# Products of the full array split into two row halves that work side by side on two token tiles

## The chip, the cores and the metric

One core of a Trainium2 chip runs the kernel. The metric is the device time of one execution in microseconds (us). The kernel before takes 2042.18 us (median of three runs, 2042.11 to 2042.24). Its engines: TensorE (PE in the rows; PEld is its loading of stationary operands), VectorE (DVE), ScalarE (ACT), GpSimd (POOL) and SyncE (SP), which issues the large transfers.

## The reference

A trunk of two layers over 256 tokens of 2048 numbers in float32, each layer a mixer and an MLP, each with an RMS norm ahead and a residual sum behind:

```python
for layer in range(DEPTH):                       # DEPTH = 2
    h = rmsnorm(x, norm_mix_w[layer])
    if layer % 2 == 0:   # retention (8 heads) and RG-LRU (8 blocks) behind one input product
        y = hybrid_mixer(h, hyb_w_in[e], ..., hyb_w_out[e], pos)
    else:                # windowed attention, 32 query heads, 4 key heads, learned sinks
        y = swa_sink_attention(h, attn_w_qkv[o], attn_sinks[o], attn_w_out[o])
    x = x + y
    h = rmsnorm(x, norm_mlp_w[layer])
    u = jax.nn.relu(h @ w_up)                    # 2048 x 8192
    x = x + (u * u) @ w_down                     # 8192 x 2048
return rmsnorm(x, final_norm_w)
```

Nearly all the arithmetic is weight products of [256 x 2048] by [2048 x 512] pieces.

## The kernel before, in words

**Blocks.** The weight products are cut into 89 blocks (`BLOCKS`): each takes all 2048 rows of contraction and 512 output columns, for both token tiles (`tt` 0 and 1, 128 tokens each). A block is 8 halves (`HALVES`), each half is 256 rows of contraction, two steps `e` of 128 rows: 712 halves in all. The two token tiles accumulate in two banks of PSUM, `acc[:, b % 2, tt]`; the other two of `acc` belong to the neighbouring block.

**Three products for one.** Weights and activations are kept as a high part and a low part in a rounded 32-bit format (`w_hi`, `w_lo`; `a_hi`, `a_lo` or `b_hi`, `b_lo`). Each step is hi x hi, hi x lo and lo x hi (L1040, L1041, L1042). So a half has 2 steps x 2 token tiles x 3 = 12 products, each with a stationary 128x128 piece of the activations and 512 streamed weight columns.

**How a half comes in.** SP loads 1 MB of weights (two halves) into one of four places of `raw` (L420), ACT rounds a half into `w_hi` (`cut_hi`, L537), DVE subtracts to get `w_lo` (`cut_lo`, L722) and raises `lo_ready`. `w_hi` and `w_lo` are rings of four halves (`RING = 4`). `cut_hi` waits for `half_used`, which TensorE raises at the end of each half. ACT and DVE run the same list of slots: in slot `b`, at each position `k` of 0 to 7, first what is left over from block `b - 1` (`post`, `lru`, `retention`, `attention`), then the cut of half `k + 4`. Each engine works strictly in this written order.

**What is left over from a block.** After an "up" block (MLP, first product) ACT takes the sums out, applies ReLU and squares; DVE transposes 32x32 tiles (L908), 4 at position 1 and 6 at each of positions 2 and 3; then ACT and DVE write the high and low parts. After a "res" block DVE adds into `x` and does the same transposes. "down" blocks only add into `x`. In the mixers and in attention TensorE itself transposes (`turn_block`, L1051; L1140) and computes scores and values between the halves (L1084, L1085: gates of the LRU; L1095, L1096: retention's scores; L1105 to L1107: its values; L1130: attention's scores; L1154: its values). These use full rows, except L1130, whose operands have 64 rows and 64 columns, and L1154, with 64 columns. Most of these small ones are plain 32-bit matmuls that the compiler issues as two each. `retention` on DVE waits for the scores at positions 2 and 3 and makes `ret_decayed`; rotation of q and k is L767 to L772.

**The loops.** Six of eight chunks of the two MLPs run in a loop on each engine (`run_slots`); two blocks at the joint from up to down are woven (`WOVEN`, `piece`).

Of the kernel before, what the change touches and what calls it, by code (L numbers as in the profile page):

```python
# [28 lines left out]
P = 128  # L29
# [4 lines left out]
TT = SEQ // P  # L34
# [5 lines left out]
CHUNK = 64  # L40
# [4 lines left out]
LRU_BLOCKS = 8  # L45
LG = LRU_BLOCKS // 2
# [11 lines left out]
UNITS = 4  # L58
HALVES = 8
RING = 4  # L60
# [20 lines left out]
MIX_OUT0 = len(MIX_IN)  # L81
# [4 lines left out]
PERIOD = 2 * COLS  # L86
# [20 lines left out]
def piece(b, k):  # L107


    for first in (b, b - 1):  # L110
        if first in DOWN0:
            d, h = WOVEN[HALVES * (b - first) + k]
            return first + d, h
    return b, k
# [77 lines left out]
def row_groups(b):  # L192


    return [0, 2, 3, 1] if MIX_OUT0 <= b < MIX_OUT0 + COLS else [0, 1, 2, 3]
# [20 lines left out]
def build(nc, t):  # L216
    ctx = ExitStack()
    with ctx:
        def sb(name, shape, dt=F32):
            return ctx.enter_context(nc.sbuf_tensor(name, shape, dt))  # L220

        def sem(name):
            return ctx.enter_context(nc.semaphore(name))
# [3 lines left out]
        w_hi = sb("w_hi", [P, RING, 2, NB], F32R)  # L227
        w_lo = sb("w_lo", [P, RING, 2, NB], F32R)
# [70 lines left out]
        acc = ctx.enter_context(nc.psum_tensor("acc", [P, 2, TT, NB], F32))  # L299
# [13 lines left out]
        hi_ready = sem("hi_ready")  # L313
        lo_ready = sem("lo_ready")
        half_used = sem("half_used")
        evac_act = sem("evac_act")
        evac_dve = sem("evac_dve")
        squared = sem("squared")
# [4 lines left out]
        turned_out = sem("turned_out")  # L323
# [24 lines left out]
        lru_lo = sem("lru_lo")  # L348
# [36 lines left out]
        def stationary(b):  # L385

            from_b = (MIX_OUT0 <= b < MLP0 or ATT_OUT0 <= b < MLP1
                      or BLOCKS[b][0] == "down" or (b >= MLP0 and BLOCKS[b][0] in ("res", "fin")))
            return (b_hi, b_lo) if from_b else (a_hi, a_lo)
# [637 lines left out]
        def _(pe):  # L1027
            def products(slot, k):

                b, h = piece(slot.b, k)  # L1030
                hi, lo = stationary(b)
                pe.wait_ge(lo_ready, slot.halves(k + 1))
                for e in range(2):
                    kt = 4 * row_groups(b)[h // 2] + 2 * (h % 2) + e
                    wh, wl = w_hi[:, k % RING, e, :], w_lo[:, k % RING, e, :]
                    first, last = h == 0 and e == 0, h == HALVES - 1 and e == 1
                    for tt in range(TT):
                        xh, xl = (s[:, kt, tt * P:(tt + 1) * P] for s in (hi, lo))
                        a = acc[:, b % 2, tt, :]
                        nc.tensor.matmul(a, xh, wh, start=first, stop=False)  # L1040
                        nc.tensor.matmul(a, xh, wl, start=False, stop=False)  # L1041
                        ins = nc.tensor.matmul(a, xl, wh, start=False, stop=last)  # L1042
                ins.then_inc(half_used, 1)

            def turn_block(src, banks):

                for m in range(2):
                    for e in range(2):
                        for tt in range(TT):
                            c = (2 * m + e) * P  # L1050
                            ins = nc.tensor.transpose(  # L1051
                                bank[:, banks + m, e * SEQ + tt * P:e * SEQ + (tt + 1) * P],
                                src[:, tt, c:c + P], ident[:, :])
                    ins.then_inc(turned, 1)

            def post(slot):

                b = slot.b - 1
                kind, j = BLOCKS[b]
                if kind not in TURNED - BY_QUADRANT:  # L1060
                    return
                if kind in FROM_STAGE:
                    pe.wait_ge(evac_act, slot.count(N_EVAC_ACT, 0))
                    src = stage
                elif kind in "qk":
                    pe.wait_ge(rotated, {("q", 0): 1, ("k", 0): 2, ("q", 1): 3, ("k", 1): 4}[(kind, j)])
                    src = turn
                else:
                    pe.wait_ge(gated, TT * (j + 1))
                    pe.wait_ge(ret_evac, TT * (j + 1))  # L1070
                    src = turn
                if kind == "aq" and j > 0:
                    pe.wait_ge(att_lo, TT * j)
                pe.wait_ge(turned_out, slot.count(N_TURNED, -1, INIT_HALVES))
                turn_block(src, 0)
# [35 lines left out]
            def retention(half, k):  # L1111
                for what, h in {1: [(ret_score, 0), (ret_score, 1)],
                                2: [(ret_value, 0), (ret_score, 2), (ret_value, 1), (ret_score, 3)],
                                3: [(ret_value, 2), (ret_value, 3)]}.get(k, []):
                    what(half, h)
# [43 lines left out]
            def attention(g, k):  # L1159
                late = att_late(g)  # L1160
                for what, tt in {1: [(att_scores, 0)], 2: [(att_scores, 1)],
                                 4 + late: [(att_turn, 0), (att_turn, 1)],
                                 5 + late: [(att_value, 0), (att_value, 1)]}.get(k, []):
                    what(g, tt)
# [11 lines left out]
            def body(slot):  # L1176
                b = slot.b
                if b == NBLK:
                    return
                if b >= 2:  # L1180

                    if BLOCKS[b - 2][0] in BY_ACT:
                        pe.wait_ge(evac_act, slot.count(N_EVAC_ACT, -1))
                    else:
                        pe.wait_ge(evac_dve, slot.count(N_EVAC_DVE, -1))
                if b in STATIONARY_STARTS:
                    pe.wait_ge(turned_out, slot.count(N_TURNED, -1, INIT_HALVES))
                for k in range(HALVES):
                    if b == 0:
                        pe.wait_ge(turned_out, k + 1)  # L1190
                    if b == MIX_OUT0 and k in (2, 5):
                        pe.wait_ge(lru_lo, LRU_BLOCKS - 1 + k // 5)
                    if b == ATT_OUT0 and k == 0:
                        pe.wait_ge(att_lo, TT * (KV - 1))
                    if b == ATT_OUT0 and k == HALVES - 2:
                        pe.wait_ge(att_lo, TT * KV)
                    if b in STATIONARY_STARTS - DOWN0 and k == HALVES - 2:
                        pe.wait_ge(turned_out, slot.count(N_TURNED, 0, INIT_HALVES))
                    if b in DOWN0 and k == HALVES - 2:
                        pe.wait_ge(evac_act, slot.count(N_EVAC_ACT, 0))  # L1200
                    if b - 1 in DOWN0 and k == HALVES - 4:
                        pe.wait_ge(turned_out, slot.count(N_TURNED, -1, INIT_HALVES))
                    products(slot, k)
                    if b == 0 and k == 5:

                        pe.wait_ge(vecs_loaded, 144)
                        pe.wait_ge(turned_out, INIT_HALVES)
                        nc.tensor.transpose(bank[:, 2, 0:4 * KT], vec_rows[0:4 * KT, 0, :], ident[0:4 * KT, 0:4 * KT])
                        nc.tensor.transpose(bank[:, 2, 4 * KT:136], vec_rows[0:72, 1, :],
                                            ident[0:72, 0:72]).then_inc(vecs_turned, 1)  # L1210
                    if b == 0 and k in (1, 3):
                        j = 2 + k // 2
                        pe.wait_ge(x_loaded[j], 16)
                        pe.wait_ge(turned_out, 2 * (j - 1))
                        turn_block(x[:, :, j * NB:(j + 1) * NB], 2 * (j % 2))
                    if b > 0:
                        kind, j = BLOCKS[b - 1]
                        if k == TURN_AT.get(kind):
                            post(slot)
                        if slot.i is None:  # L1220
                            if kind == "v":
                                retention(j, k)
                            if b in LRU_IN_SLOT and k == 4:
                                lru_gates(LRU_IN_SLOT[b])
                            if kind == "aq":
                                attention(j, k)

            run_slots(pe, body)


# [22 lines left out]
```

## Time and profile before

| | |
|---|---|
| median of 3 runs | 2042.18 us |
| the profiled execution | 2042.25 us, span 2040.4 us |
| PE busy | 2006.0 us, 98% |
| PEld busy | 1655.3 us, 81% |
| DVE busy | 1422.7 us, 70% |
| ACT busy | 1019.6 us, 50% |
| POOL busy | 43.3 us, 2% |
| DMA | 187 GB/s over the span |

A matmul's recorded duration (0.39 us for a product) includes its way through the array; a stream of them starts one every 0.227 us, so the busy times overlap. The time between starts is the cost of one in a stream.

### The profile page before, as it was taken

Reading aid. Unit: us, or ns where it says so; the run is one execution under the profiler, and the core shown is the slowest. Engines: PE = TensorE matmul, PEld = TensorE weight load, DVE = VectorE, ACT = ScalarE, POOL = GpSimd, SP = SyncE. Lnnn points to the kernel's source line nnn. Section 1 sums busy time; section 2 is a strip of 40 time slices with the busy share of each in tenths; the row PEclk is TensorE's granted clock in tenths of the full one; section 3 lists DMA queues with packets and bytes.
Section 4 is the critical chain, followed back from the end, with each engine's and each line's share of the span. In section 5 each row is a group of like instructions: output and inputs, shape, how many; then the busy total and the mean of one; then the engine's idle time right before and its main releaser. Section 6 shows DMA issues by size and latency. Waiting matters only on the chain.

```text
span 2040.4 us, 24588 instructions
## 1 busy us (share of the span) xinstructions
PE 2006.0 (98%) x9195; PEld 1655.3 (81%) x9195; DVE 1422.7 (70%) x1931; ACT 1019.6 (50%) x1343; POOL 43.3 (2%) x55
## 2 busy tenths in 40 slices
PE   8999999999999999999999999999999999999997
PEld 6888888878888888888887877878888888888876
DVE  5776678887567657756888677978548756855864
ACT  5566665555345435434555554555445434534543
POOL 1110110000000000000000000000000000000000
PEclk9999999999999999999999999999999999999999
DMA  8556546656656665556656544566656566566552
GB/s 292 171 169 210 175 156 208 198 171 206 194 180 204 198 192 189 201 186 194 197 173 199 165 133 156 181 193 192 200 188 195 193 191 196 182 204 193 186 192 97
DMA packets 191612, 382.49 MB, mean 187 GB/s; under 512 B 6184, under 2 KB 6448, under 8 KB 191408
## 3 DMA queue, kind: packets, MB, share of 16 engines
q1 hardware_dynamic: 190288, 377.58, 57.1%
q0 software_dynamic: 1216, 3.88, 0.5%
q8 instruction: 49, 0.80, 0.2%
q14 instruction: 27, 0.22, 0.0%
q10 hardware_dynamic: 32, 0.01, 0.0%
HBM read 379.34 MB, written 2.10 MB: 187 GB/s over the span
## 4 chain that ended last, share of the span: by engine, by line
PE 89%; DVE 6%; ACT 3%; issue 1%; DMA 0%; ACTq 0%; SPq 0%; DVEq 0%
PE acc L1040 29%; PE acc L1042 29%; PE acc L1041 29%; DVE w_lo L722 2%; DVE turn L908 2%; ACT w_hi L537 1%; PE bank L1051 1%; PE bank L1130 0%; DVE a_lo L734 0%; ACT L601 0%; PE bank L1140 0%; PE bank L1154 0%; ACT area L627 0%; DMA x<-in_x 0%; ACT L607 0%
## 5 line engine op out<-in xcount | busy, mean ns | idle before, releaser
L722 DVE TENSOR_TENSOR w_lo<-raw,w_hi 128x1024 fp32r<-128x1024 f32 x712 | 867.1, 1225 | 550.5 <-ACT w_hi L537 548.0
L537 ACT ACTIVATE w_hi<-raw 128x1024 fp32r<-128x1024 f32 x712 | 748.2, 1059 | 835.6 <-PE acc L1042 835.3
L1040 PE MATMUL acc<-w_hi,a_hi 128*128 128x512 f32 x1568 | 616.3, 393 | 5.0 <-DVE a_lo L734 4.7
L1042 PE MATMUL acc<-w_hi,a_lo 128*128 128x512 f32 x1568 | 611.2, 390 | 0.0
L1041 PE MATMUL acc<-w_lo,a_hi 128*128 128x512 f32 x1568 | 611.0, 390 | 0.0
L1040 PE MATMUL acc<-w_hi,b_hi 128*128 128x512 f32 x1280 | 499.0, 390 | 4.9 <-DVE b_lo L730 2.6
L1042 PE MATMUL acc<-w_hi,b_lo 128*128 128x512 f32 x1280 | 498.0, 389 | 0.0
L1041 PE MATMUL acc<-w_lo,b_hi 128*128 128x512 f32 x1280 | 498.0, 389 | 0.0
L1040 PEld LDWEIGHTS acc<-w_hi,a_hi 128*128 128x128 f32 x1568 | 295.0, 188 | 68.8 <-DVE a_lo L734 6.0
L1042 PEld LDWEIGHTS acc<-w_hi,a_lo 128*128 128x128 f32 x1568 | 294.8, 188 | 61.9
L1041 PEld LDWEIGHTS acc<-w_lo,a_hi 128*128 128x128 f32 x1568 | 295.0, 188 | 60.1
L1040 PEld LDWEIGHTS acc<-w_hi,b_hi 128*128 128x128 f32 x1280 | 240.3, 188 | 56.4 <-DVE b_lo L730 3.5
L1042 PEld LDWEIGHTS acc<-w_hi,b_lo 128*128 128x128 f32 x1280 | 240.3, 188 | 50.2
L1041 PEld LDWEIGHTS acc<-w_lo,b_hi 128*128 128x128 f32 x1280 | 240.3, 188 | 49.6
L908 DVE STREAM_TRANSPOSE turn<-stage 32x256 f32<-32x256 f32 x512 | 223.1, 436 | 7.7
L545 ACT ACTIVATE b_hi<-turn 128x512 fp32r<-128x512 f32 x64 | 37.0, 625 | 101.1 <-DVE turn L908 101.1
L908 DVE STREAM_TRANSPOSE turn<-x 32x256 f32<-32x256 f32 x192 | 83.6, 436 | 2.9
L582 ACT ACTIVATE stage<-acc,rinv 128x512 f32<-128x512 f32 x92 | 57.6, 674 | 1.4 <-DVE rinv L755 1.4
L929 DVE TENSOR_TENSOR x<-x,acc 128x512 f32<-128x512 f32 x80 | 51.1, 680 | 8.6 <-PE acc L1042 8.6
L730 DVE TENSOR_TENSOR b_lo<-turn,b_hi 128x512 fp32r<-128x512 f32 x64 | 41.2, 685 | 0.0
L587 ACT ACTIVATE stage<-stage 128x512 f32<-128x512 f32 x64 | 36.7, 627 | 0.0
L555 ACT ACTIVATE junk<-x 128x512 f32<-128x512 f32 x40 | 25.0, 624 | 11.8 <-DVE x L929 11.1
(152 smaller groups left out, 522.6 us busy)
## 6 DMA issues: line engine op xcount, KB each, us to landing
raw<-in_mlp_w_up SPq DMA_DIRECT2D x128, 1024.0 KB, 5.6
raw<-in_mlp_w_down SPq DMA_DIRECT2D x128, 1024.0 KB, 5.1
raw<-in_hyb_w_in SPq DMA_DIRECT2D x48, 1024.0 KB, 5.1
raw<-in_attn_w_qkv SPq DMA_DIRECT2D x20, 1024.0 KB, 5.1
raw<-in_hyb_w_out SPq DMA_DIRECT2D x16, 1024.0 KB, 5.3
raw<-in_attn_w_out SPq DMA_DIRECT2D x16, 1024.0 KB, 5.1
x<-in_x SPq DMA_DIRECT2D x4, 512.0 KB, 9.7
out_y<-x SPq DMA_DIRECT2D x4, 512.0 KB, 4.0
```

The source lines that it names most:

```text
L537: nc.scalar.activation(w_hi[:, h % RING], raw[:, h // 2, 2 * (h % 2):2 * (h % 2) + 2, :], ACT.Copy).then_inc(hi_ready, 1)
L545: nc.scalar.activation(hi[:, kt:kt + 2, :], src, ACT.Copy).then_inc(turned_hi, 1)
L555: nc.scalar.activation(junk[:, :], x[:, tt, j * NB:(j + 1) * NB], ACT.Square, accum_out=sums[:, norm, tt, j:j + 1]).then_inc(summed, 1)
L582: ins = nc.scalar.activation(stage[:, tt, :], src, ACT.Relu if kind == "up" else ACT.Copy, scale=s)
L587: nc.scalar.activation(stage[:, tt, :], stage[:, tt, :], ACT.Square).then_inc(squared, 1)
L722: nc.vector.tensor_tensor(w_lo[:, h % RING], raw[:, h // 2, 2 * (h % 2):2 * (h % 2) + 2, :], w_hi[:, h % RING].bitcast(F32), ALU.subtract) ...
L730: nc.vector.tensor_tensor(lo[:, kt:kt + 2, :], src, hi[:, kt:kt + 2, :].bitcast(F32), ALU.subtract).then_inc(turned_out, 1)
L908: ins = nc.vector.transpose(dst[f * QUAD:(f + 1) * QUAD, :, :, a, :], src[a * QUAD:(a + 1) * QUAD, :, :, f, :])
L929: nc.vector.tensor_tensor(xs, xs, acc[:, b % 2, tt, :], ALU.add).then_inc(evac_dve, 1)
L1040: nc.tensor.matmul(a, xh, wh, start=first, stop=False)
L1041: nc.tensor.matmul(a, xh, wl, start=False, stop=False)
L1042: ins = nc.tensor.matmul(a, xl, wh, start=False, stop=last)
```

## The change

`products` is called for even `k` only and handles two halves. Each product is now two matmuls of 64 rows: the upper 64 rows (side 0) work on one token tile and the lower 64 (side 1) on the other. After both halves the sides exchange token tiles and all is gone through again with the other rows of the same weights. The order of the two turns alternates, so that the last turn of one pair of halves and the first of the next have the same assignment. Ahead of the second turn TensorE waits for `rows_done`, raised by the last matmul of each side. `half_used` is raised in the second turn. `lo_ready` is asked for two halves at once. Work that is posted at an odd position `k` on TensorE stands behind the pair.

```diff
+        rows_done = sem("rows_done")
@@ products
-                b, h = piece(slot.b, k)
-                hi, lo = stationary(b)
-                pe.wait_ge(lo_ready, slot.halves(k + 1))
-                for e in range(2):
-                    kt = 4 * row_groups(b)[h // 2] + 2 * (h % 2) + e
-                    wh, wl = w_hi[:, k % RING, e, :], w_lo[:, k % RING, e, :]
-                    first, last = h == 0 and e == 0, h == HALVES - 1 and e == 1
-                    for tt in range(TT):
-                        xh, xl = (s[:, kt, tt * P:(tt + 1) * P] for s in (hi, lo))
-                        a = acc[:, b % 2, tt, :]
-                        nc.tensor.matmul(a, xh, wh, start=first, stop=False)
-                        nc.tensor.matmul(a, xh, wl, start=False, stop=False)
-                        ins = nc.tensor.matmul(a, xl, wh, start=False, stop=last)
-                ins.then_inc(half_used, 1)
+                q = k // 2
+                pe.wait_ge(lo_ready, slot.halves(k + 2))
+                for turn_no, swap in enumerate((0, 1) if q % 2 == 0 else (1, 0)):
+                    if turn_no == 1:
+                        pe.wait_ge(rows_done, slot.plus(2 * (UNITS * slot.b + q) + 2, 2 * UNITS * PERIOD))
+                    for m in range(2):
+                        b, h = piece(slot.b, k + m)
+                        hi, lo = stationary(b)
+                        for e in range(2):
+                            kt = 4 * row_groups(b)[h // 2] + 2 * (h % 2) + e
+                            for n, (s, w) in enumerate(((hi, w_hi), (hi, w_lo), (lo, w_hi))):
+                                for side in range(2):
+                                    tt = side ^ swap
+                                    rows = slice(side * CHUNK, (side + 1) * CHUNK)
+                                    ins = nc.tensor.matmul(
+                                        acc[:, b % 2, tt, :], s[rows, kt, tt * P:(tt + 1) * P],
+                                        w[rows, (k + m) % RING, e, :],
+                                        start=h == 0 and (turn_no, e, n) == (0, 0, 0),
+                                        stop=h == HALVES - 1 and (turn_no, e, n) == (1, 1, 2))
+                                    if turn_no == 0 and (m, e, n) == (1, 1, 2):
+                                        ins.then_inc(rows_done, 1)
+                        if turn_no == 1:
+                            ins.then_inc(half_used, 1)
@@ body
-                    if b == 0:
-                        pe.wait_ge(turned_out, k + 1)
-                    if b == MIX_OUT0 and k in (2, 5):
-                        pe.wait_ge(lru_lo, LRU_BLOCKS - 1 + k // 5)
+                    if b == 0 and k % 2 == 0:
+                        pe.wait_ge(turned_out, k + 2)
+                    if b == MIX_OUT0 and k in (2, 4):
+                        pe.wait_ge(lru_lo, {2: LG, 4: LRU_BLOCKS}[k])
...
-                    products(slot, k)
+                    if k % 2 == 0:
+                        products(slot, k)
```

On TensorE, the middle of a pair of halves: before, the end of one half and the start of the next (L1040 to L1042 are the three products).

```order
L1040 MATMUL acc<-w_hi,a_hi 128x512
L1041 MATMUL acc<-w_lo,a_hi 128x512
L1042 MATMUL acc<-w_hi,a_lo 128x512
L1040 MATMUL acc<-w_hi,a_hi 128x512 [waits lo_ready]
L1041 MATMUL acc<-w_lo,a_hi 128x512
L1042 MATMUL acc<-w_hi,a_lo 128x512
```

After, the same place, the exchange (all products are L1049 there; x2 is the upper and the lower rows).

```order
L1049 MATMUL acc<-w_hi,a_hi 128x512 x2
L1049 MATMUL acc<-w_lo,a_hi 128x512 x2
L1049 MATMUL acc<-w_hi,a_lo 128x512 x2
L1049 MATMUL acc<-w_hi,a_hi 128x512 [waits rows_done]
L1049 MATMUL acc<-w_hi,a_hi 128x512
L1049 MATMUL acc<-w_lo,a_hi 128x512 x2
L1049 MATMUL acc<-w_hi,a_lo 128x512 x2
```

The wait for a weight half went to every second half, and in the middle TensorE waits for its own matmuls.

On TensorE, the slot after a "v" block, retention's values (L1105 to L1107 before) and its last score (L1095, L1096). Before, the second pair of values stands behind another half:

```order
L1095 MATMUL bank<-area 128x256 [waits ret_decayed]
L1096 MATMUL bank<-area 128x128
L1040 MATMUL acc<-w_hi,a_hi 128x512 [waits lo_ready]
L1041 MATMUL acc<-w_lo,a_hi 128x512
...
L1105 MATMUL bank<-area 128x128 [waits ret_decayed]
L1106 MATMUL bank<-area 128x128
L1107 MATMUL bank<-area 128x128
```

After (the same lines are L1109, L1110 and L1119 to L1121):

```order
L1109 MATMUL bank<-area 128x256 [waits ret_decayed]
L1110 MATMUL bank<-area 128x128
L1119 MATMUL bank<-area 128x128 [waits ret_decayed]
L1120 MATMUL bank<-area 128x128
L1121 MATMUL bank<-area 128x128
```

No products stand between the last scores and the values any more. ACT, DVE and SP have the same instructions in the same order as before.

## Rows read from the trace of the kernel before

**Rows 1.** The page: busy time of engines, and the chain's shares by engine.

```profile
PE 2006.0 (98%) x9195; PEld 1655.3 (81%) x9195; DVE 1422.7 (70%) x1931; ACT 1019.6 (50%) x1343; POOL 43.3 (2%) x55
PE 89%; DVE 6%; ACT 3%; issue 1%; DMA 0%; ACTq 0%; SPq 0%; DVEq 0%
```

**Rows 2.** Waits of PE: us in total, times, longest.

```profile
PE acc L1040 <- DVE w_lo L722: 0.2, 1, 0.2
```

**Rows 3.** Windows, inside the first MLP: length, then busy us and instructions by engine, granted clock.

```profile
500.00:600.00 100.00, 100.00 (x442) 82.78 (x442) 53.18 (x51) 42.97 (x44) 0.00 (x0) 1.00 0.62 196
```

**Rows 4.** The page's groups: count, busy us, mean ns, idle before.

```profile
L722 DVE TENSOR_TENSOR w_lo<-raw,w_hi 128x1024 fp32r<-128x1024 f32 x712 | 867.1, 1225 | 550.5 <-ACT w_hi L537 548.0
L537 ACT ACTIVATE w_hi<-raw 128x1024 fp32r<-128x1024 f32 x712 | 748.2, 1059 | 835.6 <-PE acc L1042 835.3
...
L908 DVE STREAM_TRANSPOSE turn<-stage 32x256 f32<-32x256 f32 x512 | 223.1, 436 | 7.7
...
L908 DVE STREAM_TRANSPOSE turn<-x 32x256 f32<-32x256 f32 x192 | 83.6, 436 | 2.9
```

**Rows 5.** Timeline of PE, attention's scores: start us, us, instruction.

```profile
1152.72 1.10 PE L1130 MATMUL bank<-area 64*64 64x128 f32 x32
1153.75 0.50 PE L1040 MATMUL acc<-w_hi,a_hi 128*128 128x512 f32 x1
1154.09 0.40 PE L1041 MATMUL acc<-w_lo,a_hi 128*128 128x512 f32 x1
```

**Rows 6.** Lines L1130 and L1140: ns minimum/median/maximum of one.

```profile
L1130 PE MATMUL bank<-area x256: 218/269/320, 1148.7 to 1241.6; 64*64 64x128 f32 x92, 64*64 64x64 f32 x36
...
L1140 PE MATMUL bank<-ident,area x64: 270/272/328, 1162.1 to 1250.4; 128*128 128x128 f32 x64
```

**Rows 7.** Timeline of PE, attention's transposes.

```profile
1161.86 0.40 PE L1042 MATMUL acc<-w_hi,a_lo 128*128 128x512 f32 x1
1162.10 1.91 PE L1140 MATMUL bank<-ident,area 128*128 128x128 f32 x16
...
1164.07 0.39 PE L1041 MATMUL acc<-w_lo,a_hi 128*128 128x512 f32 x1
```

**Rows 8.** Timeline, all engines, a stall of PE before the mixer's output product.

```profile
323.75 1.26 DVE L734 SCALAR_TENSOR_TENSOR b_lo<-bank,vecs,b_hi 128x256 fp32r<-128x256 f32 x3
...
324.17 0.39 PE L1042 MATMUL acc<-w_hi,b_lo 128*128 128x512 f32 x1
...
325.06 0.19 PEld L1040 LDWEIGHTS acc<-w_hi,b_hi 128*128 128x128 f32 x1 [0.93 <-DVE b_lo L734]
...
325.40 0.40 PE L1041 MATMUL acc<-w_lo,b_hi 128*128 128x512 f32 x1
325.40 0.19 PEld L1042 LDWEIGHTS acc<-w_hi,b_lo 128*128 128x128 f32 x1
...
327.26 0.39 PE L1040 MATMUL acc<-w_hi,b_hi 128*128 128x512 f32 x1
```

**Rows 9.** Timeline of PE, a transpose of 64 rows after products.

```profile
32.48 0.39 PE L1042 MATMUL acc<-w_hi,a_lo 128*128 128x512 f32 x1
32.80 0.27 PE L1208 MATMUL bank<-ident,vec_rows 64*128 64x64 f32 x1
```

**Rows 10.** Timeline of DVE, slot after an "up" block.

```profile
795.07 1.78 DVE L908 STREAM_TRANSPOSE turn<-stage 32x256 f32<-32x256 f32 x4
...
804.80 1.23 DVE L722 TENSOR_TENSOR w_lo<-raw,w_hi 128x1024 fp32r<-128x1024 f32 x1
```

**Rows 11.** Windows of ACT over one group's exponentials; timeline of DVE.

```profile
1155.20:1160.95 5.75, 5.74 (x35) 1.00 0.05 18
...
1161.63 1.22 DVE L878 TENSOR_TENSOR area<-area 128x1024 f32<-128x1024 f32 x1
```

**Rows 12.** Windows of DVE over one rotation (L767 to L772).

```profile
91.40:96.40 5.00, 4.96 (x8) 1.00 0.18 69
```

**Rows 13.** Waits of the queue of SP.

```profile
SPq L420 <- DVE w_lo L722: 1807.7, 352, 12.6
```

## The prediction

> **What bounds the kernel now.** Read in this order. First the page's busy table and chain: TensorE is busy 98% of the 2040.4 us span and 89% of the chain that ended last is its own work [rows 1], so what happens to its stream of matmuls is the time. Second, who made TensorE wait: of the waits for a split weight half (L722) there is one, of 0.2 us [rows 2]; the DVE, at 70%, and ScalarE, at 50%, hide behind it. Third, a stretch in the middle of an MLP: 442 matmuls in 100 us at granted clock 1.00 [rows 3]. A matmul that only touches the edge counts too, so I take 441 steps between starts, 0.2267 us each. There are 712 weight halves (the count of L722 [rows 4]) of 12 products each, 8544 products, 8544 x 0.2267 = 1937 us. A product streams 512 columns; at the 2.4 GHz that clock 1.00 is, 0.2133 us, so at most 0.0134 us a product could be won from better overlap (114 us in all).
>
> The profiled execution took 2042.25 us, 0.07 above the median of the runs; I add to 2042.25 and do not correct.
>
> **Part 1: the halves of the array.** Each product becomes two of 64 rows, so 17088 matmuls and as many weight loads. If the two of a pair stream at the same time into their two banks, the pair costs what one product did. The nearest rows are the attention scores (L1130): 64x64 pieces on four quarters of the array, two row halves among them. 32 matmuls of 128 columns take 1.10 us from first start to last end [rows 5]; one takes 0.269, with its weights exposed 0.320 [rows 6], so 8 rounds of four span about 1.10 - 0.32 = 0.78 us, or 0.11 a round. Undivided 128-column matmuls of the same type (L1140) come 16 in 1.91 us, of 0.272 each [rows 6, 7]: (1.91 - 0.27)/15 = 0.109 apiece. So four packed ones cost what one costs, and the weight loads of the next round are hidden as they are without packing. I take 0.2267 a pair: nothing won, nothing lost. What these rows do not show: 32-bit plain matmuls move 128 columns in 0.109, half the column rate of the products, so the two-bank write at full rate is unseen. Ends: 0.2133 (gain 114 us) and, if the halves do not run together, 0.4534 (loss 1937 us).
>
> **Part 2: the exchange.** The second turn waits for rows_done, which the last two matmuls of the first turn raise. Behind that waiting weight load stands all of TensorE's program, and everyone waits for TensorE: this is bare. The rows of one stall give each piece [rows 8]. The last matmul before it runs 0.39 from its start; a release reaches TensorE's weight load 0.05 after its releaser's end (323.75 + 1.26 = 325.01, load at 325.06); from that load to the start of the next matmul's stream cadence takes 325.06 to 325.40, 0.34, since the load is no longer hidden. Last start to second start is 0.39 + 0.05 + 0.34 = 0.78 against 2 x 0.2267 = 0.45 in a running stream: 0.32 us lost. Then the stream comes back slowly: from 325.40 to 327.26 there are 8 matmuls, 1.86 us against 8 x 0.2267 = 1.81, another 0.05. There are 712/2 = 356 exchanges (the order of two turns alternates, so there is none between pairs of halves): 356 x 0.37 = 132 us. Bounds: at the low end only the reload is bare, 0.11 (a matmul with its load exposed takes 0.50 [rows 5], a hidden one 0.39 [rows 8]), 39 us. At the high end the two 64-row loads after an exchange follow one another, 0.11 more: 171 us. I take 132, since each piece is a row.
>
> **Part 3: changes of tiling.** Transposes, LRU gates and retention use 128 rows and stand between 64-row products now. A 64-row transpose after a 128-row product starts 0.32 after it (32.48 to 32.80) [rows 9], where an equal-tiled one follows in 0.24 (1161.86 to 1162.10) [rows 7]; with its own load exposed (0.320 against 0.269 [rows 6]) entering costs 0.13. Leaving: after the packed scores end (1153.82) the second product starts at 1154.09, 0.27 later [rows 5]; after L1140 (ends 1164.01) at 1164.07, 0.06 [rows 7]; 0.21 more. About 34 visits x 0.34 = 12 us (15 blocks of transposes, 3 in the first slot, 8 LRU, 4 retention, 4 of attention). The scores and values already pay.
>
> The Trainium skill (TensorEngine Tiling (Array Packing), Key Properties) says that changing the tiling mode, not merely the tile, drains the engine. The trace agrees: 0.32 against 0.24. A kernel that mixes modes as this one now does pays it at each visit; by the rule alone the sign is the same and the sum is mine.
>
> **Part 4: the ring of weight halves.** The second turn of m = 0 releases the first half, at three quarters of the pair instead of one half, and the second half only at the end; and TensorE asks for two split halves at once. I follow one slot after an "up" or "res" block, where the DVE also makes 16 transposes in its order. Time from the slot's first product, pair of halves Q = 24 x 0.2267 + 0.37 = 5.81. The first slot of the ring is free at 12 pairs (2.72) + 0.37 + 6 pairs (1.36) + 0.2 for the last matmul's tail = 4.65. ScalarE's part 1.06, the DVE's 1.23 [rows 4] and 0.1 between: 7.05. From there the DVE works without a pause through 4 transposes, cut, 6, cut, 6, cut: 795.07 to 804.80 + 1.23, 10.96 us [rows 10], so the half that TensorE asks for at 3Q = 17.43 is there at 18.0. TensorE waits 0.57, and 0.11 for the reload: 0.7. Slots: (512 + 192)/16 transposes = 44 [rows 4]; 44 x 0.7 = 31 us. Before, the first slot came free at 2.72 + 0.2 = 2.9 and the last of these cuts was asked for only at 7 x 2.72 = 19.0, which is why the wait of [rows 2] is so small. Slots after "down" blocks have no transposes and lose nothing. Bounds: 0 (if the DVE's row closes up) and 44 x 1.5 = 66 (if pairs run at 0.2158, since then 3Q is a microsecond earlier and the DVE is not).
>
> **Part 5: what is posted later.** Work that stood behind an odd half now stands behind a pair. In attention the first scores need the DVE's copies of the queries with no half between (1.3 us x 4, about); the second scores come after four halves instead of three, and behind them stand 16 exponentials of 5.75 us in ScalarE's order [rows 11], two DVE products of 1.22 [rows 11], and only then the cut of the last half: by the same adding as in part 4 that half is there about 1 us after TensorE asks for it. 4 x 2.3 = 9, and in the last group the values follow the transposes directly, 2.5 us of DVE copies: 12 us. Retention's values 2 and 3 follow scores 2 and 3 with nothing between, 1 us x 2; four rotations of 4.96 us [rows 12] stand before a cut with the tightened ring, about 0.7 each. With the first slot, which now waits for two halves, I put 18 us on this part; ends 5 and 30.
>
> **Sum:** 2042.25 + 132 + 12 + 31 + 18 = 2235 us, 9.5% slower. DMA I put at nothing: SyncE's queue sat waiting for split halves 352 times, 1808 us in all [rows 13], so a load could have been issued no sooner and has some three pairs of time to land.
>
> **The rivals.**
> A. The halves do not run together at the full column rate (the double bank write, or their streams, share a port). For it: no row shows 32-bit-rounded products packed. Against: the packed scores. 2235 + 1937 = 4172, less the ring's 31: about 4140 us.
>
> B. Weight loads are no longer hidden in row halves. The mechanism: with the same half streaming, its next load has to wait, 0.11 bare in each of 8544 pairs, 940 us: 3175 less the ring, about 3140. Against it: in the scores each quarter has its own next load, and the rounds still come at 0.11, as without packing. The Trainium skill (TensorE: Matmul & The Clock Gate, section "The mechanism" of the part on packing) says that a weight load overlaps with matmuls in flight only when the row group differs. By that rule this is what would happen; the trace of before disagrees even without tiling, where a load of the same rows starts at 325.40 with the matmul [rows 8].
>
> C. Better overlap: L1140 takes 0.1093 for 128 columns, 0.0026 over the 0.1067 of 256 ticks of 2.4 GHz, where the products are 0.0134 over theirs. If split loads bring the pair to 0.2133 + 0.0025 = 0.2158, that is -93 us; the ring then costs 66: 2177. With a cheap exchange (0.20) 2120.
>
> D. The other side. As C, but the exchange is nearly hidden because the far half still has matmuls in the array when the near one is released, and the DVE's row does not bind. In place of the sum: 8544 x 0.0134 = -114, 356 x 0.11 = +39, +12, +18: 1997. The point from which it decides, the ring at nothing: exchange below 24 x (0.2267 - pair) - 30/356; with a pair at 0.2133 that is 0.24 us, with 0.2158 it is 0.18. Against it: the rows of part 2 say 0.37 and the wait asks for both halves' last matmuls, and with shorter pairs the DVE's 18 us for three pairs of a slot binds.
>
> **Chances.** Forecast 0.79, A 0.05, B 0.04, C 0.06, D 0.06 (faster 0.04, same 0.02). A measurement of this kernel tells 0.2%, 4 us, from no change. Low end: exchange 0.32, ring and part 5 at half, 2042 + 114 + 12 + 15 + 9 = 2192, and C's 2120 taken in. High end: 171 + 12 + 44 + 30 = 2299. Range 2115 to 2300; outside lie A, B, D and some of C. Slower 0.94, same 0.02, faster 0.04.
>
> **What would show it.** The count of products' matmuls near 17088 with starts in couples a few ns apart, couples 0.227 apart; after every 12 couples a gap of about 0.6 between starts, idle charged to TensorE itself or to nobody; cuts (L722's line) among TensorE's releasers some 44 times at 0.5 us or more; TensorE busy lower than 98%. I am wrong if couples are not couples (A), if loads end before matmuls start (B), if the gap after 12 couples is below 0.45, or if the DVE's transposing slots show no wait.

## The result, and the profile after

| | before | after |
|---|---|---|
| median | 2042.14 us | 2271.36 us (2266.39 to 2273.1) |
| profiled execution, span | 2042.25, 2040.4 | 2272.51, 2270.7 |
| PE busy | 98% | 95% |
| mean granted clock of TensorE | 0.998 | 0.989 |

The ratio is 1.112, 95% interval 1.1103 to 1.1136: 229 us slower. I had forecast 2235, 193 slower, in a range of 2115 to 2300.

The page after, busy times and chain, against [rows 1]; then the instruction queue's line:

```profile
PE 2158.1 (95%) x17739; PEld 1644.5 (72%) x17739; DVE 1423.3 (63%) x1931; ACT 1021.4 (45%) x1343; POOL 42.6 (2%) x55
...
q8 instruction: 148, 2.42, 0.4%
...
PE 66%; DVE 24%; issue 5%; ACT 5%; DMA 0%; ACTq 0%; DVEq 0%; SPq 0%
```

The chain is no longer TensorE's alone: a quarter of it is DVE. The waits of TensorE after, for its loads (PEld) and matmuls (PE), against [rows 2] (us in total, times, longest):

```profile
PEld acc L1049 <- PE acc L1049: 183.1, 356, 0.8
PEld acc L1049 <- issue: 34.2, 33, 4.6
...
PE acc L1049 <- issue: 19.8, 6, 4.2
PE acc L1049 <- DVE w_lo L723: 15.4, 44, 1.5
```

There are the 356 exchanges, 44 waits for a late split half, and something that I had not named: "issue", idle time in which TensorE waited for nothing that the profile shows, up to 4.6 us. By their places, 37 of the 44 waits stand where the prediction put them, at the fourth pair of a slot behind an "up" or "res" block; the other seven are at the start of the kernel and in the slots of the mixer. One of the 37:

```profile
706.20 0.39 PE L1049 MATMUL acc<-w_hi,a_lo 64*128 64x512 f32 x2
706.82 0.50 PE L1049 MATMUL acc<-w_hi,a_hi 64*128 64x512 f32 x2 [0.23 <-DVE w_lo L723]
707.16 0.40 PE L1049 MATMUL acc<-w_lo,a_hi 64*128 64x512 f32 x2
```

The idle time in such a row counts from the end of the last record, 0.39 after its start, where the stream would have gone on after 0.227. So each wait holds the stream up by 0.16 more than its row says: here 0.62 - 0.227 = 0.39, and then 0.11 for the bare reload.

Now the timeline of TensorE over the second half of one turn and an exchange, against [rows 8] (start, us, instruction; x2 is a couple):

```profile
903.47 0.40 PE L1049 MATMUL acc<-w_hi,a_hi 64*128 64x512 f32 x2
903.70 0.40 PE L1049 MATMUL acc<-w_lo,a_hi 64*128 64x512 f32 x2
903.92 0.40 PE L1049 MATMUL acc<-w_hi,a_lo 64*128 64x512 f32 x2
904.41 0.50 PE L1049 MATMUL acc<-w_hi,a_hi 64*128 64x512 f32 x2
904.75 0.39 PE L1049 MATMUL acc<-w_lo,a_hi 64*128 64x512 f32 x2
...
906.83 0.39 PE L1049 MATMUL acc<-w_lo,a_hi 64*128 64x512 f32 x2
```

Couples start every 0.23 us, each no dearer than one undivided product. Across the exchange it is 0.49 and then 0.34 instead of 2 x 0.227, and afterwards 9 steps in 2.08 us, 0.231 each: 0.38 + 0.04 = 0.42 us an exchange here. Added up from the starts over all exchanges of this trace that ran at full clock (351 of 356; from the last couple of the first turn over the next twelve, less 12 x 0.2267) the mean is 0.39, so 140 us for 356.

The last new thing is a turn of TensorE's loop. Windows (length; busy us and instructions of PE, PEld, DVE, ACT, POOL; granted clock; DMA share; GB/s):

```profile
640.00:659.00 19.00, 18.75 (x160) 14.66 (x158) 7.35 (x6) 7.08 (x7) 0.00 (x0) 1.00 0.59 186
659.00:664.00 5.00, 1.19 (x10) 0.68 (x8) 2.45 (x2) 3.60 (x6) 0.00 (x0) 1.00 0.50 162
664.00:669.00 5.00, 4.93 (x30) 3.61 (x28) 0.00 (x0) 0.00 (x0) 0.00 (x0) 0.66 0.51 181
```

and its timeline:

```profile
659.24 0.39 PE L1049 MATMUL acc<-w_hi,a_lo 64*128 64x512 f32 x2
663.44 0.50 PE L1049 MATMUL acc<-w_hi,a_hi 64*128 64x512 f32 x2 [3.81 <-issue]
...
665.02 0.65 PE L1049 MATMUL acc<-w_hi,a_hi 64*128 64x512 f32 x2
665.45 0.65 PE L1049 MATMUL acc<-w_lo,a_hi 64*128 64x512 f32 x2
```

For 4.2 us nothing starts, and after it the granted clock of 5 us is 0.66: part of them at the lower level, 1.2 GHz, where couples start 0.43 apart. The second loop's turns are worse:

```profile
1693.10 0.39 PE L1049 MATMUL acc<-w_hi,a_lo 64*128 64x512 f32 x2
1697.70 0.79 PE L1049 MATMUL acc<-w_hi,a_hi 64*128 64x512 f32 x2 [4.21 <-issue]
...
1702.68 0.58 PE L1049 MATMUL acc<-w_hi,a_hi 64*128 64x512 f32 x1 [1.63 <-issue]
```

```profile
1693.00:1713.00 20.00, 14.07 (x78) 10.11 (x74) 5.89 (x8) 5.60 (x8) 0.00 (x0) 0.66 0.26 87
1892.00:1912.00 20.00, 13.51 (x86) 9.71 (x84) 6.35 (x8) 5.92 (x8) 0.00 (x0) 0.83 0.27 92
```

A second pause follows the first by a few microseconds (2.3 us between starts here, 2.9 at 1899.5), and the granted clock is 0.66 and 0.83 over 20 us. The DMA queues of the stretches show what happened. Before, while the loop turns (600 to 900, with a turn at 768), only the weights' queue moves; after, in 650 to 670, the instruction queue moves three packets (queue: packets, MB, share; the first fence is before, the second after):

```profile
q1 hardware_dynamic: 29210, 58.00, 59.4%
```

```profile
q1 hardware_dynamic: 1584, 3.15, 48.9%
q8 instruction: 3, 0.05, 0.9%
```

### The profile page after: what moved, and what is told of

Its sections match the earlier page's. It is cut to its first block, busy times and chain, and to the rows that moved or that the text cites. A ratio compares the mean times of both kernels' runs of the same rounds, so it can differ in the third digit from the quotient of the medians.

```text
span 2270.7 us, 41480 instructions
## 1 busy us (share of the span) xinstructions
PE 2158.1 (95%) x17739; PEld 1644.5 (72%) x17739; DVE 1423.3 (63%) x1931; ACT 1021.4 (45%) x1343; POOL 42.6 (2%) x55
## 4 chain that ended last, share of the span: by engine, by line
PE 66%; DVE 24%; issue 5%; ACT 5%; DMA 0%; ACTq 0%; DVEq 0%; SPq 0%
PE acc L1049 64%; DVE turn L909 12%; DVE w_lo L723 9%; ACT w_hi L538 3%; PE bank L1065 0%; ACT area L628 0%; PE bank L1144 0%; DVE a_lo L735 0%; PE bank L1168 0%; DMA x<-in_x 0%; PE bank L1154 0%; DVE turn L770 0%; DVE turn L768 0%; PE bank L1109 0%; PE bank L1098 0%
## 5 line engine op out<-in xcount | busy, mean ns | idle before, releaser
L723 DVE TENSOR_TENSOR w_lo<-raw,w_hi 128x1024 fp32r<-128x1024 f32 x712 | 866.9, 1224 | 770.4 <-ACT w_hi L538 758.3
L1049 PE MATMUL acc<-w_hi,a_hi 64*128 64x512 f32 x3136 | 653.6, 411 | 53.0 <-issue 19.8
L1049 PE MATMUL acc<-w_hi,a_lo 64*128 64x512 f32 x3136 | 623.7, 392 | 0.0
L1049 PE MATMUL acc<-w_lo,a_hi 64*128 64x512 f32 x3136 | 621.8, 391 | 0.0
L1049 PE MATMUL acc<-w_hi,b_hi 64*128 64x512 f32 x2560 | 522.4, 404 | 28.9 <-DVE w_lo L723 5.8
L1049 PE MATMUL acc<-w_hi,b_lo 64*128 64x512 f32 x2560 | 503.3, 388 | 0.0
L1049 PE MATMUL acc<-w_lo,b_hi 64*128 64x512 f32 x2560 | 501.3, 387 | 0.0
L1049 PEld LDWEIGHTS acc<-w_hi,a_hi 64*128 64x128 f32 x3136 | 300.0, 186 | 207.3 <-PE acc L1049 101.4
L1049 PEld LDWEIGHTS acc<-w_hi,b_hi 64*128 64x128 f32 x2560 | 241.6, 184 | 148.7 <-PE acc L1049 81.7
L1049 PEld LDWEIGHTS acc<-w_hi,a_lo 64*128 64x128 f32 x3136 | 300.7, 186 | 64.9
L1049 PEld LDWEIGHTS acc<-w_lo,a_hi 64*128 64x128 f32 x3136 | 301.7, 187 | 58.7 <-issue 5.3
L1049 PEld LDWEIGHTS acc<-w_hi,b_lo 64*128 64x128 f32 x2560 | 241.6, 184 | 51.7
L1049 PEld LDWEIGHTS acc<-w_lo,b_hi 64*128 64x128 f32 x2560 | 242.7, 185 | 44.2
```

The source lines that it names most:

```text
L723: nc.vector.tensor_tensor(w_lo[:, h % RING], raw[:, h // 2, 2 * (h % 2):2 * (h % 2) + 2, :], w_hi[:, h % RING].bitcast(F32), ALU.subtract) ...
L1049: ins = nc.tensor.matmul(acc[:, b % 2, tt, :], s[rows, kt, tt * P:(tt + 1) * P], w[rows, (k + m) % RING, e, :], start=h == 0 and (turn_no, ...
```

## The experiments

All times are medians on the chip; ratios are against the kernel before, measured beside each. The diffs are against the kernel named in the sentence ahead of each.

### Without the exchange

Against the changed kernel; it leaves out half of each product (each tile gets its own rows twice):

```diff
-                    if turn_no == 1:
-                        pe.wait_ge(rows_done, ...)
-                                    tt = side ^ swap
+                                    tt = side
```

> The changed kernel without the exchange: in both turns the upper rows stay with token tile 0 and the lower with tile 1, and rows_done is gone. The same number of matmuls and loads, but each tile gets its own rows twice and never the other's, so this leaves out half of each product. My theory (the exchange is a drain of the matmuls in flight and a bare reload, about 0.40 us at each of 356 places in the trace after): 142 us go, but pairs of halves get shorter and the split halves come late more often (now about 25 us, then about 55), so about 2165 us. Couples start 0.227 apart without a break. Rival (row halves are slow by themselves, and the exchange only stands where it is seen): the time stays above 2230 us.

2168.51 us, ratio 1.0632 (1.0614 to 1.0651): 103 us less than with the exchange. Its waits:

```profile
PE acc L1045 <- DVE w_lo L722: 60.8, 50, 2.9
```

The waits for split halves grew as expected, from 15.4 us, but not by all of the difference. Four of the 50 are the turns of the loops, which here end in a wait that the profile puts down to the DVE:

```profile
631.29 0.39 PE L1045 MATMUL acc<-w_hi,a_lo 64*128 64x512 f32 x2
634.46 0.50 PE L1045 MATMUL acc<-w_hi,a_hi 64*128 64x512 f32 x2 [2.77 <-DVE w_lo L722]
```

No other slot stops at this place, and the instruction queue moves three packets in 624 to 644 us. The four are 11.2 us, so late halves are 49.6 us. The exchange had covered 34 us of them, and some time of the other waits (a_lo 8.8 against 6.4 us). The turns also cost less in this run than in the changed kernel. So 103 plus what was covered gives the size of the exchange only roughly; the sum over its 356 places, 140 us, is the better number. The rival falls.

### Undivided products in pairs of halves

Against the changed kernel, `side` and `rows_done` gone:

```diff
-                                for side in range(2):
-                                    tt = side ^ swap
-                                    rows = slice(side * CHUNK, (side + 1) * CHUNK)
...
+                                tt = swap
+                                ins = nc.tensor.matmul(acc[:, b % 2, tt, :], s[:, kt, tt * P:(tt + 1) * P],
+                                    w[:, (k + m) % RING, e, :], ...)
```

> Undivided 128-row products in the frame of the changed kernel: two halves at a time, token tile 0 in one turn and 1 in the other, halves released in the second turn, posted work behind the pair; no rows_done, no row halves, 8544 matmuls. My theory (parts 4 and 5 of the prediction belong to the frame): with pairs of 5.44 us the slots after up and res blocks wait about 1.3 us each, 57 us, and posted work 18, so about 2115 us. Rival (the frame costs nothing, the waits for split halves in the trace after come from the row halves): under 2060 us.

2157.54 us, ratio 1.057 (1.0552 to 1.0587). The frame of pairs costs 116 us without a single row half, 42 more than expected; the rival, under 2060, falls. Its waits:

```profile
PE acc L1042 <- DVE w_lo L722: 50.0, 46, 3.1
...
PE acc L1042 <- issue: 8.0, 2, 4.0
```

Of the first, 39 waits with 41 us stand at the places forecast, 1.06 us each; with 0.16 and a reload of 0.11 for each that is 52 us, where 57 were expected. The second is two turns of the first loop, 8 us with a half clock behind each. The mean clock, 0.988, is as low as after: against the 0.998 of before that is some 20 us of the 2156, behind these turns and behind the longest stalls. What the rest of the 42 is I can't show.

### The same with a wait in the middle

```diff
+                    if turn_no == 1:
+                        pe.wait_ge(rows_done, slot.plus(UNITS * slot.b + q + 1, UNITS * PERIOD))
...
+                                if turn_no == 0 and (m, e, n) == (1, 1, 2):
+                                    ins.then_inc(rows_done, 1)
```

> As the run before it in this list, with a wait in the middle of each pair of halves for the last matmul of the first turn, which undivided products do not need. My theory: 356 drains and reloads, 142 us, of which about 30 is taken from the lateness of split halves: about 2227 us, and what is left to the changed kernel's 2271 are changes of tiling (12), the loops (16) and the slower couples (14). Rival (the drain is long only where two row halves have to end): under 2190 us.

2253.58 us, ratio 1.1032 (1.1013 to 1.105), 96 over the run without the wait, between the 2227 of my sum and the changed kernel. (The sum started from too low a frame, above, and added 112 where 96 came.) The rival, under 2190, falls. Its waits for split halves are down to 16.3 us. One drain:

```profile
701.52 0.39 PE L1046 MATMUL acc<-w_hi,a_lo 128*128 128x512 f32 x1
701.97 0.50 PE L1046 MATMUL acc<-w_hi,a_hi 128*128 128x512 f32 x1
702.31 0.40 PE L1046 MATMUL acc<-w_lo,a_hi 128*128 128x512 f32 x1
```

0.45 and 0.34: 0.34 lost, nearly the 0.32 of the prediction; the couple's 0.49 is 0.04 more. Over all the drains the difference does not even remain: added up as above, with the slower products behind it, the mean is 0.39 here too. So the row halves add nothing to the drain that shows in the time.

### TensorE's loops written out

Against the changed kernel:

```diff
-            run_slots(pe, body)
+            for b in range(NBLK + 1):
+                body(Slot(b))
```

> The changed kernel with TensorE's two loops written out (the other engines keep theirs). The trace after has four gaps of 4.2 to 4.6 us in TensorE's stream in which it waited for nothing visible, two per loop, which I did not predict. Theory: TensorE fetches its program again when a loop turns back, since the body is now twice as long; written out, the four gaps go, about 16 us: 2255 us. Rival (the gaps belong to something else in those blocks, such as a late transfer): 2271 us and the gaps stay.

2236.77 us, ratio 1.0956 (1.0938 to 1.0974): 34.6 less, twice the four gaps. The mean clock went from 0.989 to 0.996. Written out, the program still arrives in 139 packets, and no "issue" wait of TensorE is over 2.1 us:

```profile
PEld acc L1049 <- issue: 15.8, 33, 2.1
```

That turning back costs was right. What I had not counted are the second pauses in the second loop and the clock. In the trace after, the six stops are 22.6 us between starts, 21 us more than the stream; the granted clock behind them (0.84 over 11 us, twice; 0.66 and 0.83 over 20 us) is 14 us more; together 35.

### The same to the kernel before

The same edit.

> The kernel before with TensorE's two loops written out. The page's instruction queue moved 49 packets for the kernel before and none while its loops turned (581 to 957 us), so its loop body was held. Theory (fetching ahead in a straight line costs nothing, only a turn back to instructions that are no longer held does): 2042 us, no change within 3 us, with some 20 more packets. Rival (the fetches themselves cost): 2055 us or more.

2041.62 us, ratio 0.9999 (0.999 to 1.0009), with 72 packets in place of 49, arriving through the whole run. Fetching in a straight line costs nothing that can be measured here.

### Row halves in the frame of before

Against the kernel before:

```diff
-                    for tt in range(TT):
-                        xh, xl = (s[:, kt, tt * P:(tt + 1) * P] for s in (hi, lo))
...
+                    for turn_no in range(2):
+                        for n, (s, w) in enumerate(((hi, wh), (hi, wl), (lo, wh))):
+                            for tt in range(TT):
+                                r = slice(tt * CHUNK, (tt + 1) * CHUNK)
+                                ins = nc.tensor.matmul(acc[:, b % 2, tt, :], s[r, kt, tt * P:(tt + 1) * P], w[r], ...)
```

> The kernel before with each product as two matmuls of 64 rows on two token tiles and nothing else changed: one half at a time, each half released at its end, posted work where it was, no exchange. Each token tile gets its own rows twice, so half of each product is left out. Theory: couples cost what one product did (0.227), changes of tiling 12 us, and the doubled loop body turns back four times at 4.2 us with some half clock behind it, 16 to 29 us: 2075 us. Rival (row halves overlap loads better, or do so once nothing interrupts them): below 2042.

2074.1 us, ratio 1.0152 (1.0135 to 1.0169). The same window as [rows 3]:

```profile
500.00:600.00 100.00, 100.00 (x884) 82.62 (x884) 57.81 (x64) 40.23 (x39) 0.00 (x0) 1.00 0.59 196
```

884 matmuls of 64 rows where 442 of 128 stood: exactly two for one. The halves run together at the full column rate and win nothing. The 32 us are the loop turns (gaps of 3.0 to 3.8 us, four times, 13 us more than the stream) with the clock behind them (0.90, 0.80, 0.90 and 0.90 over 17 us from each, 8.5 us), and 11 us beside them, among which the changes of tiling must be. The rival, below 2042, falls.

### Cuts ahead of the transposes

Against the changed kernel with loops written out, on the DVE at positions 2 and 3:

```diff
                     cut_lo(slot, AHEAD + k)
+                    if b > 0 and BLOCKS[b - 1][0] in BY_QUADRANT and k in (2, 3):
+                        turn_quadrants(slot, k, *BLOCKS[b - 1])
```

> The changed kernel with TensorE's loops written out (2237 us) and on the DVE, at positions 2 and 3 of slots behind up and res blocks, the cut of the weight half ahead of the six transposes instead of behind them. Theory (the 46 waits for split halves, 17.6 us and a reload each, come from the transposes that stand ahead of the last cut): the waits fall to a few, 15 to 23 us less, about 2217 us. Rival (the DVE is late because ScalarE's half is released late): within 5 us of 2237.

2279.26 us, ratio 1.1162 (1.1144 to 1.1181): 42 us slower than the kernel that it changes, and my theory as stated here falls. Its waits:

```profile
ACT b_hi L546 <- DVE turn L909: 211.8, 32, 6.7
...
PE acc L1051 <- DVE w_lo L723: 38.9, 46, 1.6
```

The waits at the fourth pair of a slot are all gone, as the theory says, but 39 new ones stand at the first pair of the slot behind. My reading: the cut at position 2 has to wait for its half's release (the DVE waits for ScalarE's halves 319 times in place of 276), and the transposes had filled that time. Behind them ACT waits (211.8 us against 119.3 with the loops written out) and stands in its written order ahead of the next cuts.

### Posted work behind the pair

Against the kernel before:

```diff
-                    products(slot, k)
+                    if k % 2 == 0:
+                        products(slot, k)
+                        products(slot, k + 1)
```

> The kernel before, where TensorE runs two halves without a break (each with its own wait and release, undivided products) and does the posted transposes, scores and gates only behind the pair, as in the changed kernel. Theory: this is part 5 of the prediction alone, 10 to 20 us, about 2057 us, all of it in the two mixers. Rival (posted work is most of what the frame of pairs costs, 116 us between the kernel before and the run with undivided pairs): 2100 us or more.

2071.64 us, ratio 1.0141 (1.0124 to 1.0158): 30 us, more than the 10 to 20, and far from the rival's 2100.

```profile
PE acc L1040 <- issue: 8.2, 2, 4.2
PE bank L1051 <- DVE turn L772: 6.2, 4, 1.6
```

8 us of it are two turns of the first loop, though this program has no more matmuls than before, and 3.4 more are the clock behind them (0.90 over 17 us from each); without them it is about 18 us, as forecast. Three instruction packets move at each of these turns (in 600 to 615 and in 780 to 795). The second loop, with a body of the same length, moves none between 1531 and 1906. So a body of the old length is held or not by something beside its length, such as where it lies in the program; no run here tests what.

### Transposes spread

Against the changed kernel with loops written out:

```diff
-QUADRANTS_AT = {"up": {1: 4, 2: 6, 3: 6}, "res": {1: 4, 2: 6, 3: 6}}
+QUADRANTS_AT = {"up": {1: 4, 2: 4, 3: 4, 4: 4}, "res": {1: 4, 2: 4, 3: 4, 4: 4}}
```

> The changed kernel with TensorE's loops written out (2237 us), and the DVE's 16 transposes behind up and res blocks as 4, 4, 4, 4 at positions 1 to 4 instead of 4, 6, 6 at 1 to 3; they stay ahead of the cuts. Theory (the wait for the last split half is the DVE's own row of work ahead of it, 11 us long): that row is four transposes, 1.8 us, shorter, so the 46 waits of 0.4 us and their reloads go, 20 us, and the first blocks behind a norm, which need the last transposes, lose some 6: 2222 us. Rival (as the cut-first run suggests, ScalarE behind the transposes makes the next slots late): above 2237 us.

2229.78 us, ratio 1.0921 (1.0903 to 1.0939): 7 less, not 15.

```profile
PE acc L1049 <- DVE a_lo L735: 10.1, 3, 3.4
PE acc L1049 <- DVE w_lo L723: 5.8, 7, 1.5
```

The waits for split halves went from 46 to 7 as the theory says; part of the gain is lost where TensorE needs the last transposes (a_lo, 10.1 against 6.5 us, and b_lo), which I had put at 6. The mean clock is 0.994 where it was 0.996, another 4 us.

### Asking for one half at a time

Against the changed kernel with loops written out:

```diff
-                pe.wait_ge(lo_ready, slot.halves(k + 2))
...
+                        if turn_no == 0:
+                            pe.wait_ge(lo_ready, slot.halves(k + m + 1))
```

> The changed kernel with TensorE's loops written out (2237 us), and in the first turn the wait for a split half ahead of each half instead of for two at the start. The second half of a pair is then asked for six couples, 1.4 us, later, and it is 0.4 us late on average. Theory: the 46 waits (17.6 us) and their reloads (5 us) go, 2215 us. Rival (what is late is the first half of the pair, or the next slot's): within 5 us of 2237.

2211.08 us, ratio 1.0829 (1.0811 to 1.0847): 25.7 less. No wait for L723 is among TensorE's longest any more; the first is:

```profile
PE acc L1050 <- DVE a_lo L735: 6.4, 3, 2.1
```

### The same with undivided pairs

The same edit to the run of undivided products in pairs.

> The run of undivided products in pairs (2157 us), with the wait for a split half ahead of each half in the first turn, as in the run before it. There 46 waits took 50 us and a reload each. Theory: they shrink to nothing or nearly so and with them the half clock that follows some, 55 to 65 us less, about 2097 us. What is left above 2042 is posted work (30, with two turns of a loop) and releases in the second turn. Rival (late release alone makes the waits): above 2130 us.

2093.98 us, ratio 1.026 (1.0243 to 1.0277): 64 less. This is what remains of the frame, 52 us: posted work, 30 with its loop turns, and some 20 that I did not separate.

## Why the prediction was right, and where it was off

**Part 1, the halves of the array: right.** Couples at the full column rate, nothing won: 884 for 442. This refutes A, and C and D's gain of 93 to 114 us. It refutes B too. The Trainium skill's sentence (TensorE: Matmul & The Clock Gate, section "The mechanism") that loads overlap with running matmuls only where the row group differs does not hold here: a load of the same rows that stream ran in each couple and cost nothing. (The section also names a background weight buffer as a target that lets a load run ahead; the runs fit that, and none tests it.)

**Part 2, the exchange: right, some 6% short.** Forecast 0.37 each, 132 us; the mean over the 356 is 0.39, 140 us. The start behind the wait comes 0.48 after the last in the mean (0.49 in the rows above), where the prediction's rows give 0.39 + 0.05 = 0.44; the reload (0.11) was as read from [rows 8], and the slow restart is 0.02 to 0.03 in the mean where 0.05 was taken. (The sign that the prediction names, "about 0.6 between starts", is wider than its own rows; 0.49 is what they should have led to.)

**Part 3, changes of tiling: in keeping, not isolated.** 12 us forecast; 11 us stand beside the loop turns in the 32 us of the run with row halves only.

**Part 4, the ring: right, too large.** The mechanism is found at its place: at 37 of the 44 slots forecast TensorE waits for the split half, at five more the new stationary operands (a_lo, b_lo) come later still, and two hardly wait. (That the page counts 44 waits in all is chance.) The halves are some 0.43 us late where 0.57 was forecast, and the reload is 0.11, so these places cost 37 x 0.54 = 20 us. Taking away the demand for two at once gave 25.7 us, with the waits in the mixer; the part had 31. The dependence on the pair's length (31 us long, 66 short) is seen too: without the exchange, and with undivided pairs, the idle time at each of these places is 1.0 to 1.1 us where it is some 0.26 after. What I had wrong was how to mend it: the transposes ahead of the cut cost only where they are longer than the wait that they fill.

**Part 5, posted late: right in size.** 18 forecast, about 18 measured once the loop turns and the clock behind them are taken out.

**What was missing: TensorE's program itself.** The prediction counted "17088 matmuls and as many weight loads" and priced only their time in the array. They are also a loop body of twice the length: its 8 blocks of 8 halves of 12 products were 768 matmuls and 768 loads, and are now 1536 and 1536. The line of the page for the instruction queue was before me (49 packets), and I did not ask when they moved. Between 600 and 900 us of the kernel before, longer than one body (64 halves of 2.72 us are 174 us) and with a turn inside, none did: the body was held. After, each turn back waits 4.2 to 4.6 us for its first instructions, four times, and the pause drops the granted clock. Written out, 34.6 us go. That is nearly all of the 36 that the forecast missed: exchange 140, ring 26, tiling 11, posted work 18 and the turns 35 are 230 us, and 229 were measured. The near match is in part luck, since the terms come from different kernels. That the time still lay in the range is luck as well: its high end, 2299, was made of a dearer exchange and ring, and held no term for this.

The Trainium skill (Runtime: NRT & Kernel Launch, section "Instruction fetch mechanics") says that each engine's instructions pass through a small memory, 2048 of them for TensorE, filled in blocks of 16 KiB along the program, and that a taken branch to a target outside the current window of two blocks must fetch it before execution goes on. The trace agrees with the block (0.80 MB in 49 packets before) and with what a branch and a straight line do. It does not agree with a window of two blocks, 512 instructions: the body of the kernel before, 1536, turned back without a packet. By the 2048, 1536 instructions and what surrounds them fit, and 3072 can't; the runs agree in the two ends, and the runs with 1536 that fetched again in the first MLP say that length alone does not decide. No run here measures the size by itself.

The clock's drop in the trace after comes from two places: 14 us from the loop turns, as counted above, and 7 us from the stalls of about 2.5 us (between starts) ahead of new stationary operands (0.84 over 11 us, four times). What stays open: no run says whether an exchange once in more halves would pay; with rings of four halves it can't be tried.

No version here beats the kernel before. The best of the changed ones is 2211.08 us, and the row halves have nothing to give it: in the frame of before, with no exchange at all, they take 2074.1 us.

## What to carry to other kernels

Splitting the contraction of a full product over two row halves buys no time, since the pair streams as long as the whole. Where two parts of the array must swap accumulators, price the swap as the last matmul's full length, the release and a bare reload, about 0.4 us, and find out what it covers. Before an instruction count is doubled in a loop, look at when the instruction queue moves: a body that is held turned back for nothing here, and one that wasn't paid 3 to 6 us a turn and mostly a slow clock behind it.

## What the runs showed of the hardware that I had not expected

- A loop of TensorE that turns back to instructions no longer held stops it for 3.0 to 4.6 us in the traces here (6.4 in the run with a wait in undivided pairs), and in one program's second loop for 2 to 3 us more just behind, while the same program in a straight line runs without such a stop at 139 packets.
- After the stops of the first loop matmuls first run at 2.4 GHz and then for a while at the 1.2 GHz level, a couple every 0.43 us (clock 0.66 over 664 to 669). After the longest of the second loop they run at the lower level from the first (clock 0.66 over the 20 us from 1693).
- Two 64-row matmuls write two banks at the full column rate, 884 of them in 100 us, with both loads hidden.
